# A hybrid attention block on one Trainium2 core: forget-gate scores in two matmul passes instead of three

## The reference, cut to what matters

```python
def causal_block_attention(q, k, v, scale, cum=None):
    ...
        s = jnp.einsum('bhqd,bhkd->bhqk', qb, k, preferred_element_type=jnp.float32) * scale
        if cq is not None:
            s = s + (cq[..., :, None] - cum[:, :, None, :])
        s = jnp.where(key_pos[None, :] <= qpos[:, None], s, -jnp.inf)
        p = jax.nn.softmax(s, axis=-1)
        return jnp.einsum('bhqk,bhkd->bhqd', p.astype(v.dtype), v)
...
        log_f = jax.nn.log_sigmoid((f_logit + fox_forget_b[l]).astype(jnp.float32)).transpose(0, 2, 1)
        cum = jnp.cumsum(log_f, axis=-1)
        o_fox = causal_block_attention(fox_heads(fq), fox_heads(fk), fox_heads(fv), FOX_SCALE, cum)
```

## Time and profile before

| | us |
|---|---|
| median of 3 runs (lowest, highest) | 1874.62 (1870.64, 1875.08) |
| the profiled execution | 1877.08 |
| its span, first to last instruction | 1875.4 |
| PE busy in the span | 1793.0 (96%) |
| DVE, ACT, POOL busy | 927.9, 769.2, 337.7 |
| granted TensorE clock, mean | 0.984 |

### The profile page before, as it was taken

How to read it: one execution, slowest core, us unless ns; L and a number is a source line. 1 busy time by engine, 2 the same in 40 slices (tenths; PEclk the granted TensorE clock), 3 DMA queues, 4 the chain that set the end, 5 groups by cost and what they waited for, 6 DMA issues and landing times.

```text
span 1875.4 us, 25404 instructions
## 1 busy us (share of the span) xinstructions
PE 1793.0 (96%) x8801; PEld 1482.6 (79%) x8801; DVE 927.9 (49%) x1465; ACT 769.2 (41%) x1328; POOL 337.7 (18%) x374
## 2 busy tenths in 40 slices
PE   6799999999999999979999999999999999999998
PEld 6577777889997888757778888888787878888886
DVE  3565655556556323467455555533336455555322
ACT  4565565645455222333243333322254443333222
POOL 1333345423321000130021111101000211111000
PEclk9899999999999999989999999999999999999999
DMA  4111112112122333412323333233332333333332
GB/s 117 41 38 53 36 44 55 53 51 57 45 56 57 90 101 90 135 56 84 90 80 100 100 89 101 87 98 98 105 95 68 90 90 90 101 89 101 93 93 95
DMA packets 282071, 150.65 MB, mean 80 GB/s; under 512 B 11735, under 2 KB 277970, under 8 KB 282002
## 3 DMA queue, kind: packets, MB, share of 16 engines
q1 hardware_dynamic: 281458, 149.54, 27.5%
q0 software_dynamic: 544, 0.20, 0.1%
HBM read 147.54 MB, written 2.16 MB: 80 GB/s over the span
## 4 chain that ended last, share of the span: by engine, by line
PE 85%; DVE 8%; ACT 3%; issue 2%; DMA 1%; POOL 1%; SPq 0%; POOLq 0%; DVEq 0%; ACTq 0%
PE ps L330 65%; PE ps L846 5%; PE ps L732 3%; PE ps L1984 2%; PE ps L709 2%; PE ps L691 2%; PE ps L698 1%; ACT w_split L290 1%; DVE w_split L301 1%; PE ps L738 1%; DVE arena_r L1127 1%; PE ps L745 1%; PE ps L593 1%; DVE tmp L1577 1%; PE ps L610 1%
## 5 line engine op out<-in xcount | busy, mean ns | idle before, releaser
L330 PE MATMUL ps<-u,w_split 128*128 128x512 f32 x3888 | 928.8, 397 | 20.5 <-DVE u L1662 8.3
L330 PEld LDWEIGHTS ps<-u,w_split 128*128 128x128 f32 x3888 | 727.9, 189 | 192.0 <-issue 11.4
L301 DVE TENSOR_TENSOR w_split<-w_raw,w_split 128x1024 fp32r<-128x1024 f32 (+3 forms) x230 | 272.9, 1188 | 484.3 <-ACT w_split L290 484.3
L290 ACT CAST w_split<-w_raw 128x1024 fp32r<-128x1024 f32 (+4 forms) x321 | 288.6, 913 | 426.5 <-PE ps L330 355.7
L330 PE MATMUL ps<-arena_r,w_split 128*128 128x512 f32 x1824 | 423.1, 393 | 7.9 <-DVE arena_r L2116 3.6
L330 PEld LDWEIGHTS ps<-arena_r,w_split 128*128 128x128 f32 x1824 | 346.1, 190 | 83.0 <-DVE arena_r L2116 5.2
L1906 POOL TENSOR_TENSOR tmp<-tmp 128x512 f32<-128x512 f32 x44 | 57.1, 1298 | 425.7 <-ACT tmp L1891 425.7
L912 ACT ACTIVATE tmp<-ps,stats 128x144 f32<-128x144 f32 (+3 forms) x128 | 69.4, 542 | 149.2 <-DVE stats L1084 148.8
L301 POOL TENSOR_TENSOR w_split<-w_raw,w_split 128x1024 fp32r<-128x1024 f32 (+2 forms) x91 | 123.4, 1374 | 17.6 <-ACT w_split L290 17.3
L1550 POOL TENSOR_TENSOR tmp<-tmp 128x512 f32<-128x512 f32 x42 | 63.3, 1507 | 283.0 <-ACT tmp L1513 248.1
L846 PE MATMUL ps<-u,w_split 128*128 128x264 f32 x768 | 104.4, 288 | 0.5 <-POOL w_split L301 0.5
(11 more groups left out here) (221 smaller groups left out, 1514.5 us busy)
## 6 DMA issues: line engine op xcount, KB each, us to landing
w_raw<-in_w_in_dram SPq DMA_DIRECT2D x118, 256.0 KB, 3.1
w_raw<-in_w_ffn_gate_dram SPq DMA_DIRECT2D x88, 256.0 KB, 3.1
w_raw<-in_w_ffn_up_dram SPq DMA_DIRECT2D x88, 256.0 KB, 3.1
w_raw<-in_w_ffn_down_dram SPq DMA_DIRECT2D x64, 256.0 KB, 3.1
w_raw<-in_w_in_even_dram SPq DMA_DIRECT2D x32, 256.0 KB, 3.0
w_raw<-in_w_in_odd_dram SPq DMA_DIRECT2D x32, 256.0 KB, 3.1
w_raw<-in_w_ffn_down_dram SPq DMA_DIRECT2D x32, 192.0 KB, 2.6
w_raw<-in_w_br_mla_dram SPq DMA_DIRECT2D x16, 256.0 KB, 3.1
```

The lines of the kernel that those rows point to most:

```text
L290: ins = act.copy(dst, src)
L301: ins = dve.tensor_tensor(lo, r, hi, ALU.subtract)
L330: last = pe.matmul(out_ap, w_tile(c, ws, k - n0), moving(k, ms), start=start and n == 0, stop=stop and n == len(total) - 1, skip_group_che ...
```

## The change

For the fox pairs alone the scores are computed in two passes. Pass one (`PACKED`) contracts 128 partitions: the query's HI part stands twice, on partitions 0 to 63 and 64 to 127, against the key's HI part and, under it, the key's LO part. Pass two (`REST`) contracts 68: the query's LO part against the key's HI part, and four forget rows (two of -1 against the gate's HI and LO, and the gate's HI and LO against 1). The mask's matmul stays.

To lay this out ACT writes the query's HI part twice (four activations instead of two) and the key's HI part twice (eight copies instead of four). DVE writes as many LO parts as before, of the key to partitions 64 to 127. GpSimd does two memsets instead of five at each of two steps, and four transfers instead of two at each fox step.

```diff
         def pe_scores(pe, pr, b, fox, par, turn):
-            rows = slice(0, 97 if fox else 96 + 32 * hh)
+            rows = slice(0, 96 + 32 * hh)
...
-                    pe.wait_ge(sem(f"rows{par}"), 32 * turn + (0 if par else 32))
+                    pe.wait_ge(sem(f"rows{par}"), 64 * turn + (0 if par else 64))
...
-            q_i = [q_t[rows, slot, part, i * P:(i + 1) * P] for part in range(2)]
+            if fox:
+
+                passes = [(q_t[rows, slot, part, i * P:(i + 1) * P], k_t[rows, slot, part])
+                          for part, rows in ((PACKED, slice(0, P)), (REST, slice(0, HD + 4)))]
+            else:
+                passes = [(q_t[rows, slot, qs, i * P:(i + 1) * P], k_t[rows, slot, ks]) for qs, ks in PASSES]
...
         def act_q(act, s, c, gemm, par, kk=0, i=0):
...
-            for src, dst in q_pieces(gemm, par):
-                ins = act.copy(dst[:, HI, :], src) if gemm == "mla" else \
-                    act.activation(dst[:, HI, :], src, ACT.Copy, scale=FOX_SCALE)
+            for hh, (src, dst) in enumerate(q_pieces(gemm, par)):
+                if gemm == "mla":
+                    ins = act.copy(dst[:, HI, :], src)
+                else:
+                    for rows in (slice(0, HD), slice(HD, P)):
+                        ins = act.activation(q_t[rows, 2 * par + hh, PACKED, :], src, ACT.Copy, scale=FOX_SCALE)
...
         def act_k(act, s, c, gemm, par, kk=0, i=0):
...
-            for src, dst, cols in k_pieces(gemm, par):
+            for n, (src, dst, cols) in enumerate(k_pieces(gemm, par)):
                 ins = act.copy(dst[:, HI, cols], src)
+                if gemm == "fox":
+                    ins = act.copy(dst[:, REST, cols], src)
...
         def dve_k(dve, s, gemm, par, half):
...
-            for src, dst, cols in k_pieces(gemm, par)[2 * half:2 * half + 2]:
-                ins = dve.tensor_tensor(dst[:, LO, cols], src, dst[:, HI, cols], ALU.subtract)
+            for hh, (src, dst, cols) in enumerate(k_pieces(gemm, par)[2 * half:2 * half + 2]):
+                low = dst[:, LO, cols] if gemm == "mla" else k_t[HD:P, 2 * par + hh, PACKED, cols]
+                ins = dve.tensor_tensor(low, src, dst[:, HI, cols], ALU.subtract)
...
         def pool_rows(pool, g, par):
...
-                for n, (dst, value) in enumerate(((q_t[64:96, slots], 0.0), (k_t[64:96, slots], 0.0),
-                                                  (k_t[96:97, slots, HI, :], 1.0), (k_t[96:97, slots, LO, :], 0.0),
-                                                  (q_t[64:65, slots, HI, :], -1.0))):
+                for n, (dst, value) in enumerate(((q_t[64:68, slots, REST], -1.0), (k_t[64:68, slots, REST], 1.0))):
...
-            pool.dma_start(q_t[96:97, slots].bitcast(F32), cum[:, :, META:LEN].rearrange("(a h) j n -> a h j n", a=1)) \
-                .then_inc(sem(f"rows{par}"), 16)
-            pool.dma_start(k_t[64:65, slots].bitcast(F32),
-                           cum.rearrange("(a h) j n -> a h j n", a=1)) \
-                .then_inc(sem(f"rows{par}"), 16)
+            for j in range(2):
+                pool.dma_start(q_t[66 + j:67 + j, slots, REST].bitcast(F32),
+                               cum[:, j, META:LEN].rearrange("(a h) n -> a h n", a=1)).then_inc(sem(f"rows{par}"), 16)
+                pool.dma_start(k_t[64 + j:65 + j, slots, REST].bitcast(F32),
+                               cum[:, j, :].rearrange("(a h) n -> a h n", a=1)).then_inc(sem(f"rows{par}"), 16)
```

More of the change, by code:

```diff
@@ L214, in hybrid_blocks_kernel @@
         HI, LO = 0, 1
+        PACKED, REST = 0, 1
         PASSES = ((HI, HI), (HI, LO), (LO, HI))
@@ L686, in pe_scores @@
                 pe.wait_ge(sem("exped"), 8 * pr + b)
-            q_i = [q_t[rows, slot, part, i * P:(i + 1) * P] for part in range(2)]
+            if fox:
[3 more added lines that the diff above has]
+                passes = [(q_t[rows, slot, qs, i * P:(i + 1) * P], k_t[rows, slot, ks]) for qs, ks in PASSES]
             if i < NQ - 1:
                 n = META + n_real(b)
-                for m, (qs, ks) in enumerate(PASSES):
-                    pe.matmul(bank(B_S + i % 2, 0, n), q_i[qs], k_t[rows, slot, ks, 0:n], start=m == 0, stop=False,
+                for m, (q_i, k_i) in enumerate(passes):
+                    pe.matmul(bank(B_S + i % 2, 0, n), q_i, k_i[:, 0:n], start=m == 0, stop=False,
                               skip_group_check=True)
@@ L696, in pe_scores @@
                 for half in range(2):
-                    for m, (qs, ks) in enumerate(PASSES):
-                        pe.matmul(bank(B_S + half, 0, HALF), q_i[qs], k_t[rows, slot, ks, half * HALF:(half + 1) * HALF],
-                                  start=m == 0, stop=half == 0 and m == 2, skip_group_check=True)
+                    for m, (q_i, k_i) in enumerate(passes):
+                        pe.matmul(bank(B_S + half, 0, HALF), q_i, k_i[:, half * HALF:(half + 1) * HALF],
+                                  start=m == 0, stop=half == 0 and m == len(passes) - 1, skip_group_check=True)
                 ins = pe.matmul(bank(B_S + 1, HALF - P, HALF), ident_b[:], mask_b[:], start=False, stop=True,
@@ L1117, in dve_q @@
             else:
-                ins = dve.scalar_tensor_tensor(out=dst[:, LO, :], in0=src, scalar=FOX_SCALE, in1=dst[:, HI, :],
+                ins = dve.scalar_tensor_tensor(out=dst[:, REST, :], in0=src, scalar=FOX_SCALE, in1=dst[:, PACKED, :],
                                                op0=ALU.mult, op1=ALU.subtract)
@@ L1235, in pool_rows @@
                 pool.wait_ge(sem("pm_copied"), 8 * (g + PAIRS - 1))
-                for n, (dst, value) in enumerate(((q_t[64:96, slots], 0.0), (k_t[64:96, slots], 0.0),
-                                                  (k_t[96:97, slots, HI, :], 1.0), (k_t[96:97, slots, LO, :], 0.0),
-                                                  (q_t[64:65, slots, HI, :], -1.0))):
+                for n, (dst, value) in enumerate(((q_t[64:68, slots, REST], -1.0), (k_t[64:68, slots, REST], 1.0))):
                     pool.memset(dst.bitcast(F32), value).then_inc(sem("aug"), 1)
-                    pool.wait_ge(sem("aug"), 5 * g + n + 1)
+                    pool.wait_ge(sem("aug"), 2 * g + n + 1)
                 pool.wait_ge(sem("forget_out"), 16)
```

## The result

The changed kernel takes **1881.57 us** (median of 5 runs, 1879.41 to 1883.9). The kernel before took 1873.33 (5 runs) beside it. The ratio is **1.0042, 95% interval [1.0029, 1.0056]**: slower by 8.2 us.

The account below looks back on a forecast made before the run. PE's own queue was taken to bound the kernel, with added copies lengthening a chain of waits. 1.50 + 1.25 + 6 x 0.80 - 0.5 = +7.05 us gave 1881.7 us against the median of 1874.62, range 1875 to 1891.

Parts of the forecast that it names:

- head start: Steps 10 to 15: ACT's copy of block 2's probabilities starts 0.70 us earlier through shorter scores (bounds 0.5 and 0.77).
- A pass saves a third of the scores' time: PE, fox scores: dropping one of three passes saves 1.53 us a step, 12.3 us in steps 9 to 16.
- the lower price of about 8: By the Trainium skill page's matmul issue gaps, the passes removed would be worth about 8 us, not 12.3.
- the chain: ACT, DVE and PE waits from block 2's probabilities copy to block 7's transposes: 13.50 grows to 15.00 us, +1.50 a step.
- the smaller chain: Rival: added pieces issue faster or overlap, 0.3 to 0.7 us less in eight steps, 1876 to 1879.3 us; chance 0.22.
- The two tight points: PE, block 7: scores start 0.74 us after block 6's exponential starts, transposes 0.70 after block 6's LO copy starts.
- the 1.5 or more that was to be the sign of a right forecast: Sign: PE idle 1.5 us or more before the last scores of steps 8 to 15, released by ACT's exponential.
- Steps 8, 9 and 16: Step 8 has copies without saving, +1.50 us; step 9 saves only block 3's third, +1.25; step 16 has no copies, -0.5.
- GpSimd at nothing: GpSimd's two more transfers, up to 0.57 us each, cost nothing, at most 1.1 us in one step; fewer memsets, nothing.
- The clock rival: Rival: PE idle before block 7's scores lowers the clock; three falls add 5 us (1887), seven 12 (1893); chance 0.17.
- The rival of hidden copies: Rival: ACT's slack hides the added copies and the saved passes are won, -11.2 us, 1863.4 us; chance 0.08.
- The passes get no shorter: Rival: PE's passes do not shorten, so steps 8 to 16 lose 1.5 us each, +13, 1888 us; chance 0.03.

Follow-up runs that it names:

- pass_alone: Kernel before with the third pass of the fox scores left out, 97 partitions and ACT's copies as before: 1865.11 us against 1872.78, ratio 0.9953.
- the two runs without copies: Kernel before without the third fox pass: 1865.11 us, ratio 0.9953; changed kernel with second copies moved from ACT to GpSimd: 1865.40 us, ratio 0.9959.
- the run with still more on GpSimd: Changed kernel with the second copies of q and k taken off ACT and done by GpSimd later in the step: 1865.40 us, ratio 0.9959.
- the run with the copies alone: Kernel before with three passes, ACT copying q and k of the fox pairs a second time into unused memory: 1886.07 us against 1872.78, ratio 1.0063.
- off_sorted: Changed kernel with both second copies off ACT and the four copies of k ordered by head: 1863.86 us, ratio 0.9962.

## Why the prediction was right, and which of its terms were off

**The mechanism was right, and the total came nearer than its terms deserve.** Slower by 7.05 was forecast, and 8.37 were found in the steps, 8.2 in the medians. That the time itself, 1881.57, lies 0.1 us from the 1881.7 forecast is luck: the kernel before took 1873.33 beside the changed one and not 1874.62, and that made up for the 1.2 us that the forecast was short. Most of what it was short stands in steps 10 to 15: +0.98 us each and not +0.80, of which 0.10 is a smaller head start and 0.06 a chain that grew by 1.56 instead of 1.50.

- **A pass saves a third of the scores' time: too much.** The rows of after show it: 0.27 us for two matmuls of 144 columns where three had 0.38, 0.45 for 0.64 at 400. At 528 keys the four matmuls have 0.61, but behind a wait; without one they have 0.58 (run pass_alone) for 0.82 with six. So a removed matmul is worth 0.11 to 0.19, 0.12 at 264 columns, and some 0.1 us of a group stays. I had divided the whole by three. I had also doubled the second head's 2.30 us; the first head's blocks take 2.21. The two together make an error of 0.28 us a step (1.25, not 1.53). Eight steps of 1.25 are 10 us: between the 12.3 that the prediction let the rows decide for and the lower price of about 8 that it set against them. The head start ahead of the chain was 0.60 and not 0.70 for the same reason. In the changed kernel only that 0.10 showed, since the chain hid the rest. In the gains that I expected of the two runs without copies it did show: -11 each was expected, and -7.4 and -7.7 came, of which 2.3 us are this term (8.9 by the steps, not 11.2).
- **The chain: right in length, with two errors that cancel.** Its part from the exponential of block 5 to k was 0.99 instead of 0.65: the prediction let ACT's waits there go, but block 4's copy still waited 0.25 us for PE's transposes, which were late by PE's wait for q's LO part. I had read the waits of `pe_scores` and `pe_transposes`, and of `products_fox` only where the trace of before showed idle time. A wait that is always met leaves no row. And eight copies of k took 2.67 instead of 3.09, because every second one, which reads the partitions of the one before, starts 0.27 behind it instead of 0.39. The prediction had given shorter copies as a sign of the smaller chain; they came, and the chain was no smaller. DVE's part from the second LO part of q over block 3's copy to block 5's exponential was 0.1 longer than I took.
- **The two tight points: right.** The scores of block 7 wait for the exponential, 0.74 us after it begins (463.70 to 464.44), and block 7's transposes for block 6's copy, 0.70 after it begins (468.67 to 469.37). But the idle time ahead of the scores is 0.72 us, and not the 1.5 or more that was to be the sign of a right forecast.
- **Steps 8, 9 and 16: right** within 0.13 us each, by the same reading.
- **GpSimd at nothing: right.** Its four transfers are issued between 469.51 and 471.76, and it then still waits 4.71 us for block 0's probabilities; the run with still more on GpSimd is the faster one.
- **The clock rival did not come, and how near it was stays open.** The steps of after are at 1.00 throughout. I had put 1.6 to 1.75 us of idle time in one piece; it came as 0.68, 0.72 and 0.27 us, apart, because the unforeseen wait takes the first share. And the row of 195.55, which was followed by 0.50 in the kernel before, stands in after with the same idle time and a clock of 1.00 from 195 to 200 us. So the length of one idle time does not decide it here:

```profile
195.45 1.56 PE L795 MATMUL ps<-w_split,arena_r 128*128 128x128 f32 x12 [1.48 <-DVE tmp L1117]
```

- **The rival of hidden copies** is closed by the run with the copies alone. "The passes get no shorter" is closed by the rows above, and by off_sorted, in which the new layout has steps of 29.14 us and the kernel before 30.36.
- **What is open:** the difference between a version's steps and its medians. The pass alone gains 8.9 us by the steps and 7.7 by the medians, and the copies alone lose 12.0 and 13.3. The steps are of one execution each, with falls of the clock at other places in each; no run shows that these explain the difference.

## What to carry to other kernels

Ask of added work where it stands in its engine's queue and who is queued behind it, not how busy the engine is. ACT was busy for half of the step, and 2.0 to 2.2 us more of it cost 1.5 us in each with three passes and 2.1 with two. A saving on the engine that sets the pace is then worth only what lies ahead of the next tight wait, here 0.60 of 1.25 us. So list all waits between the edit and that point out of the code, the always-met ones too, and look for an engine off the ring (here GpSimd, and a transfer within SBUF) for work that has until the next step.

## What the runs showed of the hardware

- Two ACT copies of 64x264 out of PSUM start 0.27 us apart when the second reads the same 64 partitions as the first, and 0.39 to 0.40 when it reads the other 64, all writing to partitions 0 to 63. The four copies of q in the changed kernel, of 64x512, which switch the partitions written to each time, took 2.41 us, 0.60 each, with no such overlap, though every second one reads the same partitions as the one before. Whether the switch, the longer row or the scaled activation makes the difference was not tried.
- A transfer of 256 KB from partitions 0 to 63 to partitions 64 to 127 of SBUF, issued by GpSimd, took 0.67 us to issue and 3.0 to land (2.9 to 3.8, 8 transfers), and a GpSimd copy of 64x1056 fp32r 1.05 us.
- When one of three passes is taken away from a group of fp32r matmuls at clock 1.00, the group gets shorter by less than a third: 0.38 to 0.27 us at 144 columns, 0.64 to 0.45 at 400, 0.82 to 0.58 for six to four matmuls of 264.
- An idle time of PE of 1.47 us was followed by the lower level (0.50) in one execution, and one of 1.48 at the same place of the program by 1.00 in another.
